# Delta rule kernel: order of work re-laid, and the inverse applied to values less keys times state

## The reference, cut to what matters

```python
a = jnp.where(strict, jnp.einsum('bhnid,bhnjd->bhnij', kb, k) * decay, 0.0)
rhs = jnp.concatenate([v * beta[..., None], kb * jnp.exp(gc)[..., None]], axis=-1)
sol = lax.linalg.triangular_solve(a + eye, rhs, left_side=True, lower=True)
u, w = sol[..., :dv], sol[..., dv:]
...
def step(state, inp):
    v_new = u_c - jnp.einsum('bhcd,bhde->bhce', w_c, state)
    o = jnp.einsum('bhcd,bhde->bhce', qd_c, state) + jnp.einsum('bhij,bhje->bhie', qk_c, v_new)
    state = state * cd_c[..., None, None] + jnp.einsum('bhcd,bhce->bhde', kd_c, v_new)
```

## Time and profile before

| | us |
|---|---|
| median of 3 runs | 3094.45 (3093.21 to 3096.02) |
| profiled execution, its own time | 3094.2 |
| its span | 3092.5 |
| TensorE busy (matmul) | 2770.5, 90% |
| VectorE busy | 1607.5, 52% |
| ScalarE busy | 864.9, 28% |
| GpSimd busy | 765.5, 25% |
| granted TensorE clock, mean | 0.949 |

### The profile page before, as it was taken

One profiled execution on the slowest core, in us unless ns is written; L12 is line 12 of the kernel. 1 busy time (PEld: TensorE's weight loads), 2 busy tenths in 40 slices (PEclk: granted clock), 3 DMA queues, 4 the chain that ended last, 5 costly groups with the idle time before them and its releaser, 6 DMA issues. The chain is left out here.

```text
span 3092.5 us, 35999 instructions
## 1 busy us (share of the span) xinstructions
PE 2770.5 (90%) x13277; PEld 2301.4 (74%) x13277; DVE 1607.5 (52%) x1780; ACT 864.9 (28%) x1213; POOL 765.5 (25%) x372
## 2 busy tenths in 40 slices
PE   5788888888867999999999599999697999999996
PEld 3677777777656888888887477887576888888885
DVE  3665555655335444445444755666444455445455
ACT  4343443434233111111111434343332111111112
POOL 1332223332133122222222211111142221222213
PEclk8899999999988999999999699999898999999998
DMA  2101100100053111111111310111332111111112
GB/s 77 48 28 41 34 34 27 35 33 21 8 170 106 45 48 54 47 47 47 41 54 54 110 42 28 48 46 42 116 123 76 48 47 41 54 47 47 47 68 95
DMA packets 62891, 172.11 MB, mean 56 GB/s; under 512 B 6176, under 2 KB 23136, under 8 KB 62832
## 3 DMA queue, kind: packets, MB, share of 16 engines
q1 hardware_dynamic: 62832, 171.33, 16.5%
HBM read 146.11 MB, written 25.20 MB: 55 GB/s over the span
## 5 line engine op out<-in xcount | busy, mean ns | idle before, releaser
L151 POOL TENSOR_TENSOR f_wlo<-f_raw,f_whi 128x1024 fp32r<-128x1024 f32 x132 | 335.6, 2551 | 1080.8 <-ACT f_whi L171 1080.8
L61 PE MATMUL f_up<-x_hi,f_whi 128*128 128x512 f32 x1408 | 550.1, 391 | 22.8 <-POOL f_wlo L151 22.8
L62 PE MATMUL f_up<-x_lo,f_whi 128*128 128x512 f32 x1408 | 549.7, 390 | 0.0
L63 PE MATMUL f_up<-x_hi,f_wlo 128*128 128x512 f32 x1408 | 549.5, 390 | 0.0
L171 ACT ACTIVATE f_whi<-f_raw 128x1024 fp32r<-128x1024 f32 x132 | 139.8, 1059 | 933.6 <-PE f_up L63 505.2
L61 PEld LDWEIGHTS f_up<-x_hi,f_whi 128*128 128x128 f32 x1408 | 265.3, 188 | 78.5 <-POOL f_wlo L151 23.6
L63 PEld LDWEIGHTS f_up<-x_hi,f_wlo 128*128 128x128 f32 x1408 | 265.2, 188 | 55.2
L62 PEld LDWEIGHTS f_up<-x_lo,f_whi 128*128 128x128 f32 x1408 | 265.3, 188 | 55.1
L61 PE MATMUL f_down<-f_whi,f_hhi 128*128 128x512 f32 x704 | 277.2, 394 | 17.2 <-issue 15.6
L211 DVE TENSOR_TENSOR acc<-f_down,acc 128x512 f32<-128x512 f32 x320 | 216.9, 688 | 123.3 <-PE f_down L63 120.4
L62 PE MATMUL f_down<-f_wlo,f_hhi 128*128 128x512 f32 x704 | 276.3, 392 | 0.0
(11 more groups left out here) (356 smaller groups left out, 4843.7 us busy)
## 6 DMA issues: line engine op xcount, KB each, us to landing
f_raw<-in_ffn_w_up SPq DMA_DIRECT2D x88, 512.0 KB, 3.3
f_raw<-in_ffn_w_down SPq DMA_DIRECT2D x44, 512.0 KB, 3.3
g_raw<-in_gdn_w_in SPq DMA_DIRECT2D x32, 512.0 KB, 3.5
l_raw<-in_gla_w_in SPq DMA_DIRECT2D x26, 512.0 KB, 3.3
after_ffn_xt<-x_mid SPq DMA_DIRECT2D x16, 512.0 KB, 4.1
first_xt<-in_x SPq DMA_DIRECT2D x8, 512.0 KB, 3.3
g_columns<-cum_rows SPq DMA_DIRECT2D x8, 512.0 KB, 3.8
mixed<-g_zc SPq DMA_DIRECT2D x8, 512.0 KB, 2.8
```

The costliest lines, as they stand in the source:

```text
L61: pe.matmul(out, w_hi, x_hi, start=first, stop=False)
L62: pe.matmul(out, w_hi, x_lo, start=False, stop=False)
L63: return pe.matmul(out, w_lo, x_hi, start=False, stop=last)
L151: pool.tensor_tensor(w_lo[k][:, :], raw[k][:, :], w_hi[k][:, :].bitcast(F32), ALU.subtract) \
```

## The change

- The constants' block is gone; its GpSimd work is done inside a new `first_pass`, identity first, masks after. `first_pass` has a buffer for each of the eight input tiles and four turned tiles in PSUM.
- The w product goes. GpSimd makes `kd`, keys (by feature) times decay from the start, in place of `kb`. In the scan TensorE first multiplies keys by state (`foretold`), VectorE subtracts that from the scaled values (`value_rest`), and TensorE applies the inverse to the difference.
- TensorE's scan is laid in eighths (three matmuls) in place of fills: `foretold`, one eighth, `scan_value`, one eighth, `scan_output`, two eighths. The turning of the queries stands ahead of the last two.
- GpSimd: spreads directly after near blocks, then mask product 0, split 2, split 3, mask product 1, kd, mask product 2, keys to the end, split 4.
- VectorE: the side work is cut anew; join 0 stands ahead of `output_norm` and of the convolution of v; in head 0 the convolution of q comes directly after the coupling matrix. `key_sums` stands ahead of `mask_decay`.
- ScalarE: the output copy stands ahead of the copies for join 0 and the squares behind them; key squares and copy stand ahead of the exponentials.
- Head 0's TensorE order has fills 16 to 23 ahead of the joins and none between them; in every head one fill moves ahead of the key products.

```diff
+        RINGS = 4
+        xt = [sb(f"first_xt{c}", [P, D]) for c in range(NT)]
...
+            consts["ident_made"](pool)
+            pool.drain().then_inc(s_made, 1)
+            consts["masks_made"](pool)
...
 # GpSimd, body(h)
                 split(h, 1)
                 near_blocks(h)
-                coupling(h, 0)
-                pool.wait_ge(s_kc, h + 1)
-                pool.tensor_tensor(kb[:, :, :], kt[:, :, :], wide(hg[:, G_CUM_EXP, :]), ALU.mult).then_inc(s_kb, 1)
-                split(h, 2)
                 spread(h, 0)
                 spread(h, 1)
-                if not peeled(h):
-                    pool.wait_ge(s_kdp, 8 * h)
-                pool.wait_ge(s_fac, h + 1)
-                pool.tensor_tensor(kn[:, :, :], kt[:, :, :], wide(factor_end[:, :]), ALU.mult).then_inc(s_kn, 1)
+                coupling(h, 0)
+                split(h, 2)
                 if not final(h):
                     split(h, 3)
                 coupling(h, 1)
+                if not peeled(h):
+                    pool.wait_ge(s_kdp, 8 * h)
+                pool.wait_ge(s_dx, 2 * h + 2)
+                pool.tensor_tensor(kd[:, :, :], by_chunk(kT), from_start[:, :, :], ALU.mult).then_inc(s_kd, 1)
                 coupling(h, 2)
+                pool.wait_ge(s_fac, h + 1)
+                pool.tensor_tensor(kn[:, :, :], kt[:, :, :], wide(factor_end[:, :]), ALU.mult).then_inc(s_kn, 1)
...
 # ScalarE, prepare(h)
                 if not peeled(h):
+                    output_copy(h - 1)
+                m1_copies(h, 0)
+                if not peeled(h):
                     output_squares(h - 1)
                 act.wait_ge(s_qss, h + 1)
                 act.activation(stdq[:, :], ssq[:, :], ACT.Sqrt, bias=eps[:, 0:1]).then_inc(s_qstd, 1)
-                m1_copies(h, 0)
...
-                act.wait_ge(s_w, h + 1)
-                act.activation(wTn[:, :, :], by_chunk(pm), ACT.Copy, scale=-1.0).then_inc(s_wn, 1)
                 if not final(h):
+                    key_squares(h + 1)
                     decay_exps(h + 1)
-                    key_squares(h + 1)
                     key_deviation(h + 1)
...
 # VectorE
+            def value_rest(h, c):
+                dve.wait_ge(s_fp, 7 * h + c)
+                dve.tensor_tensor(rest[c % 2][:, :], vb[:, c, :], pt[:, T + HALF + P:T + HALF + 2 * P],
+                                  ALU.subtract).then_inc(s_rest, 1)
...
-                              2: lambda: near_rows(h, range(1, B // 2)),
-                              3: lambda: near_joined(h),
-                              4: lambda: near_back(h),
-                              5: lambda: conv_q(h, (1, 2)),
-                              6: lambda: conv_q(h, (3,))}
+                              2: lambda: near_rows(h, range(1, 7)),
+                              3: lambda: (near_rows(h, (7,)), near_joined(h, False)),
+                              4: lambda: (near_joined(h, True), conv_q(h, (1,))),
+                              5: lambda: near_back(h),
+                              6: lambda: conv_q(h, (2, 3))}
+                    if peeled(h):
+                        beside[0] = lambda: (coupling_matrix(h), conv_q(h, (1, 2, 3)))
...
                         update_state(h - 1, n)
+                        value_rest(h - 1, n + 1)
...
+                join(h, 0)
+                if not peeled(h):
+                    output_norm(h - 1)
                 conv_v(h, (1,))
                 if not peeled(h):
-                    output_norm(h - 1)
-                join(h, 0)
+                    output_gate(h - 1)
                 conv_v(h, (2, 3))
...
 # TensorE
+            def foretold(h, c):
+                if c:
+                    if c == 1:
+                        pe.wait_ge(s_kd, h + 1)
+                    pe.wait_ge(s_state, 7 * h + c)
+                    pe.matmul(pt[:, T + HALF + P:T + HALF + 2 * P], kd[:, c, :], state[:, :], start=True,
+                              stop=True).then_inc(s_fp, 1)
+
             def scan_value(h, c):
...
+                if c:
+                    pe.wait_ge(s_rest, 7 * h + c)
+                pe.matmul(pt[:, T:T + P], invT[:, c, :], rest[c % 2][:, :] if c else vb[:, c, :], start=True,
+                          stop=True).then_inc(s_vnp, 1)
...
             def scan(h):
                 for c in range(NT):
+                    foretold(h - 1, c)
+                    eighths(h, 4 * c, 1)
                     scan_value(h - 1, c)
-                    fill(h, 2 * c)
+                    eighths(h, 4 * c + 1, 1)
                     scan_output(h - 1, c)
-                    fill(h, 2 * c + 1)
-                queries_by_token(h)
+                    if c == NT - 1:
+                        queries_by_token(h)
+                    eighths(h, 4 * c + 2, 2)
```

More of the change, by code:

```diff
@@ new lines, in masks_made @@
+    def masks_made(pool):
+        for n, s in enumerate(sizes):
+            pool.memset(masks[:, n, :], 1.0)
+        pool.drain()
+        for n, s in enumerate(sizes):
+            blocks = P // (2 * s)
+            m = masks[:, n, :].rearrange("p (b half t) -> p b half t", half=2, t=s)
+            pool.memset(m[:, :, 0, :], 0.0)
+            for pattern, base, mult in (([[-2 * s, blocks], [0, s]], 0, 1),
+                                        ([[2 * s, blocks], [0, s]], s - 1, -1)):
+                pool.drain()
+                pool.affine_select(out=m[:, :, 1, :], in_=m[:, :, 1, :], compare_op=ALU.is_ge, fill=0.0,
+                                   base=base, pattern=pattern, channel_multiplier=mult)
@@ L661, in _ @@
[L661 to L669, removed]
@@ L670, in constants, with _, deviation, high @@
-    return dict(ident=ident, upper=upper, ones=ones, eps=eps, masks=masks)
+            consts["ident_made"](pool)
+            pool.drain().then_inc(s_made, 1)
+            consts["masks_made"](pool)
+        @block.scalar
+        def _(act):
+            def deviation(c):
+                act.wait_ge(s_x[c], 16)
+                act.activation(squares[:, :], xt[c][:, :], ACT.Square, accum_out=ss[:, c:c + 1])
+                act.drain()
+                if c == 0:
+                    act.wait_ge(s_made, 1)
+                act.activation(std[:, c:c + 1], ss[:, c:c + 1], ACT.Sqrt, scale=1.0 / D,
+                               bias=eps[:, 0:1]).then_inc(s_std, 1)
+            def high(c):
+                act.wait_ge(s_turn, c + 1)
+                act.activation(x_hi[:, :, c * P:(c + 1) * P], turned[c % RINGS][:, :, :], ACT.Copy).then_inc(s_hi, 1)
+            deviation(0)
+            deviation(1)
+            for c in range(NT):
+                if c + 2 < NT:
+                    deviation(c + 2)
+                high(c)
@@ L673, with _ @@
+        @block.tensor
+        def _(pe):
+            for c in range(NT):
+                pe.wait_ge(s_xs, c + 1)
+                if c >= RINGS:
+                    pe.wait_ge(s_lo, c - RINGS + 1)
+                for kt in range(KT):
+                    last = pe.transpose(turned[c % RINGS][:, kt, :], xs[c % RINGS][:, kt * P:(kt + 1) * P],
+                                        ident[:, :])
+                last.then_inc(s_turn, 1)
 GDN_HEADS = 8
@@ L1422, in fill, with eighths @@
                 for n in some:
-                    if final(h) and n >= 24:
+                    eighths(h, 2 * n, 2)
+            def eighths(h, start, count):
+                for n in range(start, start + count):
+                    if final(h) and n >= 48:
                         return
-                    k, half, part = n // 8, n // 4 % 2, n % 4
+                    k, half, kt_ = n // 16, n // 8 % 2, n % 8
                     s = slot(k)
                     cols = slice(half * HALF, (half + 1) * HALF)
-                    if part == 0:
+                    if kt_ == 0:
                         pe.wait_ge(s_lo, begun(h, k))
@@ L1535, in joined, with some @@
                     last.then_inc(s_x, 1)
-            def w_product(h):
-                pe.wait_ge(s_vb, h + 1)
-                pe.wait_ge(s_kb, h + 1)
-                pe.wait_ge(s_t, 2 * J * (h + 1))
-                for c in range(NT):
-                    last = pe.matmul(pm[:, c * P:(c + 1) * P], kb[:, c, :], invT[:, c, :], start=True, stop=True)
-                last.then_inc(s_w, 1)
-            def prepare(h):
+            def prepare(h):
+                def some(*fills):
+                    if not peeled(h):
+                        fill(h, *fills)
+                if peeled(h):
+                    fill(h, *range(16, 24))
                 pe.wait_ge(s_first, 2 * h + 2)
@@ L1548, in prepare @@
                 coupled(h, 0)
-                fill(h, 16)
+                some(16)
                 if not peeled(h):
```

162 lines of the change are left out of this document (102 added, 60 removed).

## The result

The changed kernel takes **3105.42 us** (median, 3103.9 to 3106.36) against 3093.98 for the kernel before, ratio 1.0034 with a 95% interval of 1.0022 to 1.0046: slower by 11 us where 11 us less were forecast. 3105.4 lies just inside the range. The profiled span went from 3092.5 to 3103.7.

What follows compares the result with a forecast made beforehand. TensorE's queue sets the pace; its waits and the half clock behind them can be won. Opening pass -14.5, opening head -10.3, loop heads +5, last head and final scan +9: -10.8, 3094.2 to 3083 us; range 3048 to 3106.

Steps and rivals of the forecast that it cites:

- Opening pass: Kernel start to the delta rule: ends about 31.2 instead of 45.7, -14.5 us; bounds -10 and -17.
- Loop head: One of six middle heads of the delta rule: 96.3 us against 95.5, +0.8; six heads +5.
- the four stalls: TensorE's waits in a loop head: first new value 1.7, last new value 6.2, normed output 6.0, next keys 1.6.
- Keys to P: Keys' turning to scan start, 6.8 against 9.7; then to P, the first coupling product, 44.0 against 41.5.
- P to C: First to second coupling product in a loop head: 20.0 us, +4.0; bounds 0 and +6.
- C to keys: Second coupling product to the turning of the next keys: 25.5 us against 28.3, -2.8.
- half clock: TensorE at the lower clock level (1.2 of 2.4 GHz): some 1.6 us lost after a stall.
- Rival B: VectorE bounds the scan, subtraction 0.7, two half-clock stretches per big stall: +4.5 a head, 3110 us; chance 24%.
- Opening head: First head of the delta rule, convolution of q first: next scan starts 10.3 us earlier; bounds -4, -17.
- The bare join chain then exposes its links: Opening head after coupled 0 (132.7): no fills cover the joins; next scan still 10.3 us earlier.
- Final scan: Nothing covers the added link: each 2.01 us chunk grows by 0.9, times seven, +6; with last head +9.
- Untouched rest: Code after the delta rule and its final scan, from 862 us, which the change does not touch: 0.

Runs made afterwards that it cites:

- e11: Changed kernel with 44 transposes of the identity, results not used, in each of the two large stalls of a head: 3080.2 us.
- e8: Changed kernel with join 1 of head 0 moved ahead of the convolution of v on VectorE: 3103.9 us.
- e13: Changed kernel with, in head 0, split 2 ahead of the spreads, join 1 ahead of the convolution of v, last coupling copies ahead of silu of v: 3082.8 us.
- e4: Changed kernel with fifteen transposes of the identity, results not used, added to each chunk of the final scan: 3095.9 us.
- e5: Changed kernel with one more wait on GpSimd: mask product 0 starts only when the convolution of q is complete: 3091.6 us.
- e12: e9 with 30 transposes added in the stall for the last new value and 20 in that for the normed output: 3032.2 us.
- e14: Changed kernel with the w product in place of the new algebra (new pass and order kept): 3059.8 us.
- e15: e10 with the head 0 moves of e13 and 24 and 16 transposes in the two stalls of a head: 2997.8 us.
- e1: The changed kernel's opening pass alone, with the delta rule as in the kernel before: 3079.4 us.
- e10: e9 with the w product in place of the new algebra and no added work in the final scan: 3021.3 us.
- e9: Changed kernel with output_norm ahead of join 0, mask product 0 behind q's convolution, head 0's split 2 early, transposes in the final scan: 3048.1 us.

## Why the prediction was wrong

- **Opening pass**: right (-15.8 for -14.5).
- **Loop head** (7.3 of the 22 us missed): the four stalls were forecast at 1.7, 6.2, 6.0 and 1.6 and came at 1.58, 5.68, 5.78 and 1.26, each at its place and with its releaser; the subtraction takes 0.29 (0.35 assumed). Keys to P took 51.2 (50.8), P to C 20.6 (20.0), C to keys 25.9 (25.5): 97.7 for 96.3. The half clock, taken as 1.6 behind each stall, is 3.7 for the two by e11; that is 0.5 of the 1.4, the rest is spread over the three legs. Against the head before, whose mean is 95.6, six of them make +12 for +5. The prediction counted two half-clock stretches in the head before (3.2 us); the trace has a third, of 3.4 us, behind the wait of 2.1 to 2.2 for the state in all six heads. Rival B named the two stretches behind a big stall, and that half of it came true; its mechanism did not: the state waits stayed under 0.9 and the subtraction at 0.29.
- **Opening head**, the step that failed most (10.7 of the 22 us missed). At the start of the scan, which the forecast named, it came to -0.6 for -10.3 (159.77 and 176.20, less the 15.8 of the pass); the table's +0.4 has 1.0 more for the first new value. That the eight fills wait for split 2 to 119.5 and coupled 0 comes at 132.7 held to 0.2 us (103.87 and 116.94, with the 15.8 of the pass added). "The bare join chain then exposes its links" was priced as the old chain less its fills: the next scan at 165.9, the keys turned 8.4 ahead of it at 157.5, which is 24.8 us behind the first coupling product. It took 35.3. The fills had hardly been in that chain: with eight of them (11.2 us) and the w product in it, it took 38.4 before. What held it were three convolutions of v between join 0 and join 1, two of them caught by GpSimd (7.5 us in all at 123.94 for 4.0 in e8), and silu of v ahead of the last copies; e13 took both out and got 28.5. The last 3.7 to the forecast were not traced.
- **Final scan**: the link was right, the clock was missed. At the upper level it adds about what was said (3.01 a chunk with transposes in e4, 2.01 without the link, forecast +0.9); but the whole scan ran at the lower level, a chunk took 4.0 and the scan grew by 12.7 and not by 6. It did not fall there because of the link: the clock was low at the first chunk before as well (832.5 to 839.3, behind a wait of 2.26 at 831.34), and without the link it rose within two chunks. With the link it never rose, in none of the nine kernels that have the link and no added work there. The last head before it was 2.3 shorter and not 3 longer, which hid the error in the sum (+10.3 for +9): that part of the agreement is luck.
- **Untouched rest**, +4.1, forecast 0. From the next block's first product to the end, the seventeen kernels took 2215.4 to 2221.9 us with the same code, low stretches falling at other places; e4, which differs only in the final scan, has 2216.7, the changed kernel 2220.4 and the one before 2216.4. What puts a kernel at one end was not settled. The five kernels that keep w took 2215.4 to 2216.8 and the twelve with the algebra 2216.7 to 2221.9; no run says whether that is more than chance.
- **What the sum hid.** The prediction set the algebra's cost on VectorE (0.95 a chunk, 6.6 a head) against the blocking that the new order of GpSimd removes, some 5 a head, and had them nearly cancel. For the kernel as a whole that was about right: keys to P took 51.2 for 50.8. But one of the two is a choice. With w kept, the new order alone is worth 20 us, and the algebra on top of it costs 45.6, since it pushes the last convolution of the queries back by 4.7 us and behind the mask product, and holds the final scan at the lower clock. Reading the diff as two changes would have shown one to keep and one to drop.

Two pages of the Trainium skill were tried by these rows. "ScalarE: Activation LUTs", section "What ACT_TABLE_LOAD costs", adds a drain of 1.38 to each load that switches the set; after the change again a load of 1.28 follows the activation ahead of it at once (305.99 and 1.06 long, then 307.06) and is followed by the root at 308.36. The measurement decides: no drain here. "SBUF — State Buffer", section "SBUF: two separate sides", says that VectorE and GpSimd share one pair of ports as an exclusive lock: an instruction of GpSimd and one of VectorE with two inputs in SBUF exclude each other, and whichever starts first holds the pair to its end. The trace agrees, both ways: the convolution ended 1.08 after the mask product (295.42 and 294.33), and the mask product itself took 3.32 because it started inside the convolution before it, against 2.37 when alone (e5).

## What to carry to other kernels

Price a change that has two ideas as two changes, each with and without the other (here the algebra cost 21 us in the old order and 46 in the new), and put a new link of a recurrence against everything that hangs on the engine it goes through, not against the matmuls that it saves. Where waits of TensorE of 2 us and more remain, add to each what the half clock costs behind it, or fill them with work whose result is not used; that was worth 25 us in the changed kernel (waits of 5.7) and 16 in e12 (waits of 3.8 and 2.8). When cover is taken from a chain, follow the chain itself through every queue before subtracting the cover.

## What was not expected of the hardware

- What a wait costs beside its length comes in steps. In the loop heads of the seventeen kernels no low stretch followed any of the 196 waits of 1.0 to 1.7 us; behind waits of 2.1 to 3.9 there was one of 3.4 us in 86 cases, none in 24 and one of 6.8 in 4; behind waits of 5.3 to 5.8 it was 6.8 us in 75 cases and 3.4 in 15, and began inside the wait.
- One added link decided which level a chain of short products ran at. The final scan begins at 0.50 in all kernels but e14 and e15. Without the link the clock rose within two chunks (before, e1, e10); with it the scan stayed at 0.50 from end to end although TensorE's products fill 22.2 of 27.97 us, and with five transposes in each gap it rose within the first chunk (e4, e9, e12). In e11, whose loop heads ran at 1.00 throughout, it fell to 0.50 at 804.9 behind a wait of 2.36 ahead of the scan, and stayed there.
- Moving a GpSimd product away from one VectorE step hands the collision to the next product in its queue at the same price (3.11 and 3.10 us), until GpSimd is made to wait.
